# Two decoder layers on one core: output projection by token halves, stick heads in pairs, and other lags and rings

## What is computed

```
for layer in range(2):
    shift, scale, gate = split(silu(c) @ w_mod[layer] + b_mod[layer], 3)
    hdn = rms_norm(x, norm_w[layer]) * (1 + scale) + shift
    q1, k1, v1, g1, q2, k2, v2, g2 = split(hdn @ w_in[layer], 8)      # 512 columns each
    if layer == 0:
        y1 = diff_attention(q1, k1, v1)      # group A: 4 heads, p0 - lam * p1, then an rms norm (subln)
        y2 = dilated_attention(q2, k2, v2)   # group B: 8 heads
    else:
        y1 = moba_attention(q1, k1, v1)      # group C: 8 heads
        y2 = stick_breaking_attention(q2, k2, v2)   # 8 stick heads, no norm on q, k
    y = concat(y1 * silu(g1), y2 * silu(g2)) @ w_out[layer]
    x = x + gate * y
```

## Time and profile before

| | |
|---|---|
| median of 3 runs | 361.4 us (360.02 to 362.07) |
| profiled execution | 359.28 us |
| its span, first to last instruction | 357.2 us |
| TensorE (PE) busy | 304.9 us, 85% |
| VectorE (DVE) busy | 261.6 us, 73% |
| ScalarE (ACT) busy | 203.9 us, 57% |
| GpSimd (POOL) busy | 15.9 us |
| loaded | 68.95 MB |
| mean granted TensorE clock | 0.962 |

### The profile page before, as it was taken

One profiled execution on the slowest core, in us unless ns is written; L12 is line 12 of the kernel. 1 busy time (PEld: TensorE's weight loads), 2 busy tenths in 40 slices (PEclk: granted clock), 3 DMA queues, 4 the chain that ended last, 5 costly groups with the idle time before them and its releaser, 6 DMA issues.

```text
span 357.2 us, 4940 instructions
## 1 busy us (share of the span) xinstructions
PE 304.9 (85%) x1741; PEld 250.5 (70%) x1741; DVE 261.6 (73%) x533; ACT 203.9 (57%) x400; POOL 15.9 (4%) x20
## 2 busy tenths in 40 slices
PE   4278796888785999979991789999999999989995
PEld 4156575666564888868770568878889788978884
DVE  2697788976978599899986758568776554558674
ACT  3435518663465575888615255647675577696920
POOL 0000061000000044000000000000000000000000
PEclk9999989998999899999997589999999999999999
DMA  7999997465464455747794305455656655300002
GB/s 268 367 418 397 375 347 273 172 237 198 163 229 168 184 195 208 275 151 260 265 347 140 107 1 194 161 177 184 228 178 191 223 176 176 119 0 3 0 31 88
DMA packets 19880, 70.32 MB, mean 197 GB/s; under 512 B 2192, under 2 KB 2576, under 8 KB 19856
## 3 DMA queue, kind: packets, MB, share of 16 engines
q1 hardware_dynamic: 19856, 70.01, 55.0%
HBM read 68.95 MB, written 1.05 MB: 196 GB/s over the span
## 4 chain that ended last, share of the span: by engine, by line
PE 44%; DVE 37%; ACT 11%; issue 6%; DMA 1%; SPq 0%; ACTq 0%; DVEq 0%
PE proj L953 30%; DVE w_lo L651 11%; DVE raw L667 11%; PE score L953 7%; ACT w_hi L409 3%; PE mixed L953 2%; PE turned L998 2%; DVE y L861 1%; PE turned L980 1%; ACT probs L505 1%; DVE logits L747 1%; ACT y L429 1%; DVE gt L821 1%; DVE y L829 1%; DVE n_ms L778 1%
## 5 line engine op out<-in xcount | busy, mean ns | idle before, releaser
L651 DVE TENSOR_TENSOR w_lo<-raw,w_hi 128x1024 fp32r<-128x1024 f32 x80 | 96.7, 1221 | 19.3 <-ACT w_hi L409 19.3
L953 PE MATMUL proj<-w_hi,hy_hi 128*128 128x512 f32 x176 | 75.4, 428 | 16.7 <-DVE w_lo L651 13.2
L409 ACT ACTIVATE w_hi<-raw 128x1024 fp32r<-128x1024 f32 x80 | 82.3, 1047 | 0.0
L953 PE MATMUL proj<-w_lo,hy_hi 128*128 128x512 f32 x176 | 72.1, 410 | 0.0
L953 PE MATMUL proj<-w_hi,hy_lo 128*128 128x512 f32 x176 | 71.8, 408 | 0.0
L667 DVE CUSTOM_DVE_ANT_0 raw<-raw,c_rows 128x1024 f32<-128x1024 f32 x48 | 59.4, 1257 | 0.0
L953 PE MATMUL proj<-hy_hi,w_hi 128*128 128x256 f32 x192 | 56.9, 296 | 0.0
L953 PEld LDWEIGHTS proj<-w_hi,hy_hi 128*128 128x128 f32 x176 | 34.7, 197 | 28.4 <-issue 16.5
L953 PE MATMUL proj<-hy_lo,w_hi 128*128 128x256 f32 x192 | 54.2, 282 | 0.0
L953 PE MATMUL proj<-hy_hi,w_lo 128*128 128x256 f32 x192 | 54.2, 282 | 0.0
L953 PEld LDWEIGHTS proj<-w_hi,hy_lo 128*128 128x128 f32 x176 | 35.1, 199 | 8.1
(11 more groups left out here) (146 smaller groups left out, 398.6 us busy)
## 6 DMA issues: line engine op xcount, KB each, us to landing
raw<-in_w SPq DMA_DIRECT2D x80, 512.0 KB, 4.4
raw<-in_w_mod SPq DMA_DIRECT2D x48, 512.0 KB, 3.9
xs<-in_x SPq DMA_DIRECT2D x1, 1024.0 KB, 5.3
out_x<-xs SPq DMA_DIRECT2D x4, 256.0 KB, 2.0
cst<-in_constants SPq DMA_DIRECT2D x1, 520.0 KB, 7.7
logits<-in_a_lambda SPq DMA_DIRECT2D x1, 128.0 KB, 12.0
rows<-in_vectors SPq DMA_DIRECT2D x1, 64.0 KB, 1.8
cst<-in_constants SPq DMA_DIRECT2D x1, 64.0 KB, 2.1
```

The lines of the kernel that those rows point to most:

```text
L409: nc.scalar.activation(w_hi[:, n % PIECES, :, :], raw_tile(("w", n)), ACT.Copy).then_inc(hi_done, 1)
L651: nc.vector.tensor_tensor(w_lo[:, n % PIECES, :, :], raw_tile(("w", n)), w_hi[:, n % PIECES, :, :], ALU.subtract).then_inc(lo_done, 1)
L953: return nc.tensor.matmul(o, a, b, start=start, stop=stop, skip_group_check=True)
```

## The change

- The 16 steps of the output projection are ordered by token half: 8 steps for half 0, then 8 for half 1 (before: the first two row blocks for both halves, then the last two by halves). The next layer's K1 and Q1 are ordered by halves as well, and the steps at which x is squared, normalised and turned move.
- `PIECES` (rings w_hi, w_lo) 6 to 8, `RAW` 10 to 7; pieces are split 8 steps ahead instead of 6, or as soon as the ring allows.
- In the first blocks the first weight of a block is split before the block's y; c's rows are turned by transposes instead of matmuls, and their second half is copied after the seed.
- Group A's first map is not normalised: the second is scaled by lam times the ratio of the sums, and the output by the first inverse sum (two ScalarE copies instead of one). Group B's scaling moves from VectorE to ScalarE (`scale_map`).
- Maps are turned one step later (4 and 5 after the scores, was 3 and 4). Gate tiles go through in lags 2, 3, 4 (was 2, 4, 6).
- Stick heads run in pairs, every fifth step, in the two score banks, with their matmuls interleaved.
- Half of the second layer's h is made by ScalarE; the normalised x by VectorE. The bias tiles of GpSimd share memory with qn and start after Q2 has been turned.

```diff
-RAW = 10
-PIECES = 6
+RAW = 7
+PIECES = 8
...
-        out += [(K1, p, s) for s in range(2) for p in range(4)]
-        out += [(c, p, s) for c in (Q1, V1) for p in range(4) for s in range(2)]
+        out += [(c, p, s) for s in range(2) for c in (K1, Q1) for p in range(4)]
+        out += [(V1, p, s) for p in range(4) for s in range(2)]
...
-    out += [(c, p, s) for c in (O0, O1) for p in range(2) for s in range(2)]
-    out += [(c, p, s) for s in range(2) for c in (O0, O1) for p in (2, 3)]
+    out += [(c, p, s) for s in range(2) for ps in ((0, 1), (2, 3)) for c in (O0, O1) for p in ps]
...
-LATE = {36: 66, 37: 67, 38: 69, 39: 70, 40: 72, 41: 74, 42: 77, 43: 78}
...
-    return FIRST[n] - 6
+    if n < 12:
+        return FIRST[n] - 6
+    return max(FIRST[n] - 8, LAST[n - PIECES] + 1)
...
-STICK_AT = 42
-X_AT = (78, STEPS + 1)
+STICK_AT, STICK_EVERY = 42, 5
+X_SQUARE, X_SEED, X_AT = (70, 72, 78, 80), (73, 81), (74, 83)
...
-    return 5 if group(j) == 0 else 6
+    return 6 if group(j) == 0 else 7
...
             def first_blocks(p):
+                split_hi(3 * p)
                 key, b = ("first", p), (turned, mixed)[p % 2]
...
+                for n in range(3 * p + 1, 3 * p + 3):
+                    split_hi(n)
...
+            def scale_map(j, o):
+                M = 2 * j + o
+                act.wait_ge(inv_ok, M - 7)
+                for tile, cs in enumerate((slice(0, P), slice(P, MAPW))):
+                    i = nc.scalar.activation(probs[:, M % 4, cs], probs[:, M % 4, cs], ACT.Copy,
+                                             scale=stat[:, M % 4, 4 + tile:5 + tile])
+                i.then_inc(prob_ok, 1)
...
                 take_scale(0, 2 * p, 2)
+                split_lo(3 * p)
                 h_lo(p + 1, slice(2 * p, 2 * p + 2), slice(0, S))
-                for n in range(3 * p, 3 * p + 3):
+                for n in range(3 * p + 1, 3 * p + 3):
                     split_lo(n)
...
             pool.wait_ge(cst_in, 16)
+            wait_turned(pool, ("qk", 0, Q2, 1))
...
-                if lag == 4:
+                if lag == 3:
...
-                if lag == 6:
+                if lag == 4:
```

More of the change, by code:

```diff
@@ L178, in turned_at @@
     out += [("subln", i) for i in range(2) if layer == 0 and SUBLN_AT[i] == g]
-    out += [("probs", j, 1) for j in pairs_at(layer, g, 3) if group(j) == 0]
-    out += [("probs", j, o) for o in range(2) for j in pairs_at(layer, g, 3 + o) if group(j)]
+    out += [("probs", j, 1) for j in pairs_at(layer, g, 4) if group(j) == 0]
+    out += [("probs", j, o) for o in range(2) for j in pairs_at(layer, g, 4 + o) if group(j)]
     out += [("x", t) for t in range(2) if X_AT[t] == STEPS * layer + g]
@@ L189, in mixed_at @@
     out = [("pair", j) for j in range(PAIRS) if PAIR_AT[j] + pv_lag(j) == at]
-    out += [("stick", m // 2) for m in sticks_at(layer, g, 6) if m % 2]
+    out += [("stick", i) for i in sticks_at(layer, g, 6)]
     out += [("gate", layer, c) for c in range(2) if GATE_ROWS[layer] + c == at]
@@ L205, in mixed_by_scalar @@
 def mixed_by_scalar(key):
-    return key[0] in ("pair", "stick", "gate", "first")
+    return True
 def turned_free(key):
@@ L440, in _ @@
             square_x(0, 0, slice(0, D), junk[0])
-            for half in range(2):
-                act.wait_ge(c_T, half + 1)
-                nc.scalar.activation(c_rows[:, half * CH:(half + 1) * CH], proj[half][:, :], ACT.Copy).then_inc(c_ok, 1)
+            act.wait_ge(c_T, 1)
+            nc.scalar.activation(c_rows[:, 0:CH], proj[0][:, :], ACT.Copy).then_inc(c_ok, 1)
             act.wait_ge(x_sq, 1)
@@ L449, in _ @@
             first_blocks(0)
-            for n in FIRST_SPLITS:
-                split_hi(n)
             act.wait_ge(vec_c, 2)
@@ L595, in _ @@
[L595 to L599 removed]
+                    for o in range(2):
+                        for j in pairs_at(layer, g, 3 + o):
+                            if group(j) == 1:
+                                scale_map(j, o)
@@ new lines, in _ @@
+                    for i in sticks_at(layer, g, 5):
+                        act.wait_ge(d_tri, i + 1)
+                        wait_mixed(act, ("stick", i - 2) if i >= 2 else ("pair", 10 + i))
+                        for o in range(2):
+                            nc.scalar.activation(probsT[:, (2 * i + o) % 4, :], score[o][:, 0:MAPW], ACT.Exp).then_inc(d_a, 1)
+                    for i in sticks_at(layer, g, 1):
+                        act.wait_ge(stick_ok, i + 1)
+                        if i:
+                            act.wait_ge(d_sp, 2 * i)
+                        for o in range(2):
+                            nc.scalar.activation(logits[:, o, :], score[o][:, 0:MAPW], ACT.Abs).then_inc(d_abs, 1)
+                        act.wait_ge(d_abs, 2 * i + 2)
+                        nc.scalar.activation(logits[:, :, :], logits[:, :, :], ACT.Exp, scale=-1.0).then_inc(d_exp, 1)
+                        act.wait_ge(d_exp, i + 1)
+                        nc.scalar.activation(logits[:, :, :], logits[:, :, :], ACT.Ln, bias=1.0).then_inc(d_ln, 1)
@@ L601, in _ @@
+                    for i in sticks_at(layer, g, 3):
+                        act.wait_ge(d_sp, 2 * i + 2)
+                        if i:
+                            act.wait_ge(d_tri, i)
+                        slots = slice(2 * (i % 2), 2 * (i % 2) + 2)
+                        nc.scalar.activation(sp_hi[:, :, :], probs[:, slots, :], ACT.Copy).then_inc(d_hi, 1)
                     for c, s in tiles_done(layer, g):
```

199 lines of the change are left out of this document (94 added, 105 removed).

## The result

The changed kernel takes 350.77 us (median of 4 runs, 348.91 to 351.85); the kernel before took 360.82 on the same chip (360.02 to 362.07). The ratio is 0.971, with a 95% interval of 0.9675 to 0.9744: faster by 10 us, where 27.6 were forecast. The profiled execution, the fastest of the four, took 348.91, 10.4 less than the one of before, and its last matmul ends at 343.17 instead of 353.28, so 10.1 of the 10.4 lie in the stages. Executions more than 1.5% above the fastest of their kernel are left out of all ratios, and the profile of experiment 9 (347.17 us) is of such a one.

A forecast was written before the change was run, and what follows sets the result against it. No one engine bounds all of the kernel. Stage terms -7.3 - 0.5 - 8.5 + 1.7 - 13.2 + 0 - 1.4 + 1.6 sum to -27.6 us, giving 331.7 profiled or 333.8 by the median, range 327 to 341.

The forecast's parts named there:

- the start: Up to step 18: reordered first-block splits, GpSimd's bias work moved away and one c copy off the chain save 7.3 us.
- PE without these gaps keeps its clock: Steps 24 to 45: with shorter map waits the clock stays up, worth 3.4 us, of which 2.0 was taken.
- no more than 8.5: Steps 24 to 45: gain capped at 8.5 us, to 49.0, as VectorE's 43.3 is just over PE's floor.
- idle of 7 to 8% gives 42.0: Steps 46 to 63: three engines at 36 to 39 us, plus idle, make the stage 42.0, +1.7.
- Half 1 has four steps (5.5) for 5.1, nothing lost: Steps 64 to 83: half 1's chain of 5.1 us fits within four PE steps of 5.5, so no wait.
- the early end of half 0: Steps 64 to 83: half 0 of O done after step 71, x turned after 74; stage 35.0 us, -13.2.
- the last stage: Steps 144 to 159: early need of G2's tiles loses 1.6 us, giving 23.5.
- Logits of a pair: Steps 122 to 143: interleaved stick heads cost 1.27 us a pair, not 2.12; 3.4 saved, floor 46.2.
- the signs: Step 18 at 49 to 50; second-map waits below 3 us; first turn under 2.5; ScalarE 37 or more in steps 46 to 63.
- The rival with ScalarE as the bound: B pairs 48 us, boundary 38.5, sticks 55, last stage 25; 18 less gained, 352 in all; chance 0.15.
- The rival of the boundary: Eight splits in VectorE's stream at steps 74 to 81 keep the turn waiting; 8 us more, 342; chance 0.10.
- the signs of being wrong: VectorE waits for raw tiles, the B stage takes over 46 us, or the first turn still waits over 5.

The follow-up runs named there:

- experiment 9: Changed kernel with the output projection's old order in layer 1 alone and Q1's four splits at steps 79, 80, 82, 83; ratio 0.9502 to the kernel before.
- experiment 11: Changed kernel with the old order of splits in the first blocks; ratio 0.9868 to the kernel before.
- experiment 14: Kernel of experiment 9 plus G1's old gate lags in layer 0, with later w_mod products cut to a quarter of their width; 330.88 us, ratio 0.915.
- experiment 2: Changed kernel with group B's scaling back on VectorE; ratio 0.9758 to the kernel before.
- 10: Kernel of experiment 9 with the old gate lags for G1's tiles in layer 0 alone; 342.1 us, ratio 0.9477 to the kernel before.
- 5: Changed kernel with the old gate lags for G1's tiles in layer 0 alone; ratio 0.9701 to the kernel before.
- 7: Changed kernel with the output projection in its old order in both layers and the old steps for x; ratio 0.9553 to the kernel before.
- 13: Kernel of experiment 9 plus G1's old gate lags in layer 0, without GpSimd's work (group B's dilated bias left out); 342.04 us, ratio 0.9464.
- 12: Changed kernel with group B's old map lags, its scaling on VectorE and G1's old gate lags in layer 0; ratio 0.9839 to the kernel before.
- 3: Changed kernel with the splits of Q1's four pieces of layer 1 at steps 81 to 84 instead of 77 to 80; ratio 0.9685 to the kernel before.
- 6: Changed kernel with the splits of Q1's four pieces of layer 1 at steps 79, 80, 82 and 83; ratio 0.9618 to the kernel before.

## Why the prediction was wrong in size, step by step

**Right: the start.** 6.9 of the 7.3 us, and experiment 11 shows that the place of the splits brings 5.1 of it. (A block's 10.2 us in the working should be 10.4, 11.5 less 1.1, or 353 GB/s; no other term hangs on it.) VectorE in the second block after (start, us, instruction, idle before):

```profile
26.45 1.22 DVE L677 TENSOR_TENSOR w_lo<-raw,w_hi 128x1024 fp32r<-128x1024 f32 x1
28.34 0.69 DVE L725 TENSOR_TENSOR hy_lo<-y,hy_hi 128x512 fp32r<-128x512 f32 x1 [0.68 <-ACT hy_hi L435]
29.30 2.36 DVE L677 TENSOR_TENSOR w_lo<-raw,w_hi 128x1024 fp32r<-128x1024 f32 x2 [0.26 <-ACT w_hi L409]
```

The wait of 1.81 in the earlier trace rows is filled with a w_lo, and 0.68 is left. Loads came into sight: ScalarE waited four times for a raw tile, 12.2 us in all, but each time ahead of a split that VectorE took later. The page's rate row of after:

```profile
GB/s 258 370 413 354 374 354 384 183 246 212 187 209 242 124 236 249 127 241 361 203 160 180 294 12 174 139 180 237 184 199 237 147 152 217 78 62 0 0 62 60
```

Its third slice, 413, and the 392 of steps 18 to 23 are above the 358 that the Trainium skill gives for a core, as half of what a stack of memory gives two cores ("SBUF — State Buffer", section "A bandwidth-pool intuition that's wrong"); here one core runs, and the measurement decides, as it did in the earlier trace rows.

**Right in kind, short in size: steps 24 to 45** (51.85 for 49.0). The wait for the second map went, even more than forecast, 9.0 to 1.8, but all waits of PE in the stage only from 9.7 to 6.3, since others came. "PE without these gaps keeps its clock" did not hold: half clock from 85.3 to 88.7, 1.7 us. And "no more than 8.5" rested on VectorE's 43.3 of work fitting in 49.0: it was busy 42.61 in 51.85. With the w_mod products cut (experiment 14) the stage took 46.99 at full clock.

**The step that failed: "idle of 7 to 8% gives 42.0"** for steps 46 to 63. The loads were forecast well: VectorE 39.0, measured 38.33; ScalarE 37.5, measured 39.25. (The 16 scalings were put at 4.5 from a range whose lower end, 0.25, no row shows; taking them away in experiment 2 took 5.3.) But the stage took 46.91, with its busiest engine idle for 16% of it. I had taken the busiest engine and a share of idle; each engine is in turn late for another, because each takes its work in program order. The chain that ends in PE's wait of 4.86, on ScalarE:

```profile
145.76 0.79 ACT L519 ACTIVATE probs<-probs,stat 128x128 f32<-128x128 f32 x2
148.28 0.63 ACT L652 ACTIVATE hy_hi<-y 128x512 fp32r<-128x512 f32 x1 [1.74 <-DVE y L862]
148.82 1.04 ACT L409 ACTIVATE w_hi<-raw 128x1024 fp32r<-128x1024 f32 x1
149.77 0.47 ACT L477 ACTIVATE probsT<-turned 128x384 f32<-128x384 f32 x1
```

PE has one bank for turned maps, and can turn the next only when ScalarE has copied the last out of it (`probsT`). That copy stands behind a split and behind the high part of a gate tile, which waits 1.74 us for VectorE's product (at 147.56), which stands behind a w_lo and a w_mod tile on VectorE:

```profile
143.89 1.22 DVE L677 TENSOR_TENSOR w_lo<-raw,w_hi 128x1024 fp32r<-128x1024 f32 x1
145.02 1.22 DVE L693 CUSTOM_DVE_ANT_0 raw<-raw,c_rows 128x1024 f32<-128x1024 f32 x1
146.16 0.09 DVE L693 DVE_READ_ACCUMULATOR2_ANT v<- 128x1 f32 x1
```

The 4.9 us too much divide so: 2.75 are the w_mod products in VectorE's stream (44.73 to 41.98 in experiment 14), and 2.2 the shorter gate lags, 1.2 of them longer waits and the rest half clock (46.91 to 44.73 or 44.80 in experiments 10 and 5). What remains, 42.0, is 37.8 of PE's steps and 4.2 of waits for ScalarE's copies. That it is the forecast's number is luck: my floor was 36.1. ScalarE is busy 38.25 of it and may be its bound; no run takes work from ScalarE alone. The earlier splits (7) are excluded as a cause, and GpSimd (13) as one of more than 0.5 us; the maps' lags (12) and the place of the scalings (2) only as causes by themselves. And the division is of the forecast's error, not of the 6.6 us by which the stage grew: the kernel before had the same w_mod products in these steps and took 40.28. What made it grow is open beyond the 2.2 of the gate lags. On GpSimd: the Trainium skill says that a VectorE instruction with two SBUF inputs and a GpSimd one that reads SBUF lock each other out ("SBUF — State Buffer", "SBUF: two separate sides"). The trace agrees so far that three VectorE instructions took 1.75 instead of 1.22. Taking GpSimd's work away took 1.75 off VectorE's busy time (36.46 to 34.71), near my 1.6, but only 0.5 off the stage.

**"Half 1 has four steps (5.5) for 5.1, nothing lost" failed** in steps 64 to 83. VectorE there, after:

```profile
184.78 3.49 DVE L677 TENSOR_TENSOR w_lo<-raw,w_hi 128x1024 fp32r<-128x1024 f32 x3
188.19 0.68 DVE L872 TENSOR_TENSOR sq<-proj,gate 128x512 f32<-128x512 f32 x1
...
191.34 1.23 DVE L677 TENSOR_TENSOR w_lo<-raw,w_hi 128x1024 fp32r<-128x1024 f32 x1 [0.60 <-ACT w_hi L409]
192.48 0.68 DVE L872 TENSOR_TENSOR sq<-score,gate 128x512 f32<-128x512 f32 x1
...
197.15 0.75 DVE L967 TENSOR_SCALAR kT<-xs,x_t 128x1024 f32<-128x1024 f32 x1
```

And PE's turn of half 1:

```profile
197.95 1.12 PE L1037 MATMUL turned<-cst,kT 128*128 128x128 f32 x4 [4.27 <-DVE kT L967]
```

PE was done with O1 of half 1 at about 188; the update from its bank began at 192.48, with w_lo after w_lo ahead. My 5.1 us were the chain alone, without the eight splits that stand in it by the same order of streams that I had read; they stood only in a rival. Experiments 3 and 6 show the price. The other terms held: turn of half 0 forecast at 1.6, measured 1.00; waits at 68 and 69 forecast at 2.8, measured 2.9. PE's own part was 31.9, not 30.6.

**What the forecast gave the wrong name to.** I let the early end of half 0 carry the boundary. Experiment 7 has the old order and a turn that waits 6.13, and still takes 41.50 of the former 48.15. So 6.7 of the 8.0 gained came with the rest of the change (the normalised x on VectorE, y on two engines, K1 and Q1 by halves, earlier splits), which experiment 7 doesn't take apart; the order itself brought 1.4, and 0.5 with steps 84 to 121 counted in. Of the 6.7, waits of PE are 2.8 (11.7 to 8.9) and half clock some 3.3 (5.2 to 2.0), which my sum had under the order's name, by going to a floor at full clock.

**Sticks and the last stage.** Logits of a pair took 1.25 us, forecast 1.27:

```profile
266.52 0.92 PE L984 MATMUL score<-qT,kT 64*128 64x256 f32 x8
267.37 0.40 PE L984 MATMUL score<-mask_tri,mask_id 128*128 128x128 bf16 x4
```

Waits were 5.4 for 4.8, of which 1.2 go with the splits that the new order of the output projection brings in here (53.34 to 52.24 in experiment 7, waits 4.2). The larger part of the 2.3 too much is PE's own work, 47.98 busy for a floor of 46.2. The last stage lost 2.8 instead of 1.6: the waits at 148 and 149 are 2.1, as forecast in kind, and the rest isn't taken apart.

**The rivals and the signs.** The rival with ScalarE as the bound named nearly these stages: 48, 38.5, 55 and 25, against 46.91, 40.12, 53.34 and 24.79. (Its parts add to 15 us less gained, 349, not to 18 and 352.) Its numbers came near, but its mechanism isn't shown: the B stage fell by 2.75 with ScalarE as busy as before (experiment 14), and at the boundary PE waited for VectorE. The rival of the boundary had the eight splits in VectorE's stream, but held them against half 0's turn; it was half 1's that waited. Of the signs, step 18, the wait for the second map, the wait of the first turn and ScalarE's load came as said. One of the signs of being wrong came too: the B stage took over 46 us.

In sum, too low were 24 to 45 by 2.9, 46 to 63 by 4.9, 64 to 83 by 5.1, sticks by 2.3, the last stage by 1.3, and the first two rows by 1.5; 84 to 121 gave back 0.5. That is 17.5 us; the profiled 348.91 misses 331.7 by 17.2, and the median 350.77 misses 333.8 by 17.0.

## What to carry to other kernels

In a kernel of in-order streams that hand work back and forth, a stage's time isn't its busiest engine plus a few per cent of idle: here the busiest was idle for 16% of it, and 2.75 us hung on an engine with 18% idle. Walk one hand-over chain through every stream it enters, with each instruction ahead of it, before giving a stage a number, and do it for the second half as well as for the first. When a reordering is one of many edits, undo it alone: the headline edit here cost about 5 us by the medians (3.8 in the profiles), and the gain was in the edits beside it.

## What the runs showed of the hardware

- The granted clock in these traces is 1.00 or 0.50 and nothing between; a fraction in a window is a mixture. Stretches at 0.50 began in a wait of PE or soon after one, and then ran on while PE was fully busy: 85.3 to 88.7 and 150.1 to 153.5 in the changed kernel, 183.9 to 190.7 in experiment 7, 191.3 to 208.4 before. The same code in steps 18 to 23 took 11.05 to 11.5 us without such a stretch and 12.5 to 13.4 with one, so stages of two kernels compare only with their clocks beside them.
- A core loaded at 392 GB/s over 11 us (steps 18 to 23), with all 16 DMA engines busy and one core running.
- fp32 work of VectorE took 1.75 us instead of 1.22 beside GpSimd's, GpSimd's own 1.71 instead of 0.73; yet taking GpSimd away changed the total by nothing that can be measured.
- The eight matmuls of two stick heads that take turns, 64 partitions each, took 0.92 us, as long as the four of one head in the kernel before:

```profile
280.39 0.92 PE L953 MATMUL score<-qT,kT 64*128 64x256 f32 x4
```
